# Three products in place of four in the block compression of a decoder layer

## The reference, cut to what matters

```python
def compress(rows, pos_emb, w1, w2):          # rows (L, 2 groups, 64); w1 (32*64, 256)
    L = rows.shape[0]
    nb = (L - CMP_BLK) // CMP_STRIDE + 1       # blocks of 32 rows, one every 16
    idx = np.arange(nb)[:, None] * CMP_STRIDE + np.arange(CMP_BLK)[None, :]
    blk = rows[idx] + pos_emb[None, :, None, :]
    blk = blk.transpose(0, 2, 1, 3).reshape(nb, KV_GROUPS, CMP_BLK * HEAD_DIM)
    return jax.nn.gelu(blk @ w1) @ w2
```

## Time and profile before

| | us |
|---|---|
| median of 3 runs | 2141.8 (2141.19 to 2146.41) |
| the profiled execution | 2143.66 |
| its span | 2142.0 |
| TensorE busy | 2000.0, 93% of the span |
| VectorE, ScalarE, GpSimd busy | 815.1, 636.2, 599.9 |
| matmuls of L1085, 1152 records | 248.2 busy |
| mean granted clock of TensorE | 0.966 of 2.4 GHz |

### The profile page before, as it was taken

How to read it: one execution, slowest core, us unless ns; L and a number is a source line. 1 busy time by engine, 2 the same in 40 slices (tenths; PEclk the granted TensorE clock), 3 DMA queues, 4 the chain that set the end, 5 groups by cost and what they waited for, 6 DMA issues and landing times. The chain is left out here.

```text
span 2142.0 us, 32815 instructions
## 1 busy us (share of the span) xinstructions
PE 2000.0 (93%) x11749; PEld 1737.9 (81%) x11749; DVE 815.1 (38%) x1590; ACT 636.2 (30%) x1290; POOL 599.9 (28%) x628
## 2 busy tenths in 40 slices
PE   6999989977999999869998889899999999999997
PEld 5777767856777777557887768699999999999987
DVE  5644443464343344466787743210111101110115
ACT  4311111112233343346777742222101111111112
POOL 0111111211222222154456631133322333223330
PEclk9999989988999999968999989999999999999999
DMA  5111101247787873470000022211111111111123
GB/s 182 50 80 40 40 12 63 83 130 115 118 105 101 100 101 55 77 135 11 11 11 21 2 99 89 71 45 43 49 49 41 47 49 43 45 49 49 45 64 120
DMA packets 173850, 141.35 MB, mean 66 GB/s; under 512 B 16602, under 2 KB 160683, under 8 KB 173411
## 3 DMA queue, kind: packets, MB, share of 16 engines
q1 hardware_dynamic: 169634, 131.43, 26.9%
q0 software_dynamic: 4096, 8.40, 2.6%
HBM read 124.27 MB, written 19.69 MB: 67 GB/s over the span
## 5 line engine op out<-in xcount | busy, mean ns | idle before, releaser
L392 PE MATMUL banks<-halves 128*128 128x344 f32 (+4 forms) x5184 | 856.5, 327 | 14.4 <-POOL halves L401 14.4
L392 PEld LDWEIGHTS banks<-halves 128*128 128x128 f32 (+1 forms) x5184 | 821.9, 188 | 45.2 <-POOL halves L401 8.0
L401 POOL TENSOR_TENSOR halves<-core,halves 128x1024 fp32r<-128x1024 f32 (+1 forms) x143 | 243.8, 1712 | 576.0 <-ACT halves L397 426.0
L392 PE MATMUL banks<-hidden 128*128 128x512 f32 (+3 forms) x1512 | 349.3, 387 | 9.0 <-DVE hidden L401 9.0
L392 PEld LDWEIGHTS banks<-hidden 128*128 128x128 f32 (+1 forms) x1512 | 254.4, 179 | 77.4 <-issue 9.6
L1085 PE MATMUL banks<-arena,blocks 128*128 128x254 f32 (+1 forms) x1152 | 248.2, 372 | 9.1 <-ACT arena L1219 5.1
L1085 PEld LDWEIGHTS banks<-arena,blocks 128*128 128x128 f32 x1152 | 209.5, 194 | 34.4 <-issue 6.1
L397 ACT ACTIVATE halves<-core 128x1024 fp32r<-128x1024 f32 (+1 forms) x85 | 88.2, 1047 | 390.2 <-PE banks L392 369.6
L2060 DVE TENSOR_TENSOR core<-banks,core 128x344 f32<-128x344 f32 x66 | 34.1, 517 | 441.0 <-PE banks L392 441.0
L1650 POOL TENSOR_SCALAR arena<-arena,kept 128x64 f32<-128x64 f32 (+8 forms) x192 | 122.9, 653 | 119.3 <-DVE arena L1702 117.7
L983 POOL DMA_DIRECT2D arena<-in_cache_kv x128 | 67.9, 530 | 232.9 <-PE banks L1129 206.0
(11 more groups left out here) (209 smaller groups left out, 1859.1 us busy)
## 6 DMA issues: line engine op xcount, KB each, us to landing
core<-in_cache_kv SPq DMA_DIRECT2D x128, 128.0 KB, 5.5
core<-in_w_gate SPq DMA_DIRECT2D x22, 512.0 KB, 3.8
core<-in_w_up SPq DMA_DIRECT2D x22, 512.0 KB, 3.8
core<-in_x_prompt SPq DMA_DIRECT2D x16, 512.0 KB, 3.4
arena<-in_cache_kv SPq DMA_DIRECT2D x128, 64.0 KB, 5.8
arena<-in_cache_kv POOLq DMA_DIRECT2D x128, 64.0 KB, 4.8
retention<-in_w_in SPq DMA_DIRECT2D x16, 448.0 KB, 6.4
core<-in_w_down SPq DMA_DIRECT2D x16, 448.0 KB, 3.7
```

The source lines that it names most:

```text
L392: done = pe.matmul(out, left[a], right[b], start=(first and i == 0), stop=(last and i == 2))
L401: return engine.tensor_tensor(lo, x, hi.bitcast(F32), ALU.subtract)
```

## The change

Write a chunk with an even number as x0 and the odd one after it as x1. The block that starts at the even chunk is W0 x0 + W1 x1, the one that starts at the odd chunk is W0 x1 + W1 x0', x0' being the next even chunk. After the change TensorE makes three products over pairs of chunks: P1 = W0 x1, P0 = W1 x0 and both = (W0 + W1)(x0 + x1). The even block is both - P1 - P0, the odd block is P1 + P0 of the next pair. Each product is 64 pairs by two groups, 128 columns (64 in the prompt), so there are 48 matmuls in place of 32.

Who does what: GpSimd adds W0 + W1 once for keys and once for values (`weight_sum`), and x0 + x1 for each of the four parts of each compression (`chunk_sums`, four additions of 128x256). TensorE multiplies the sum of part i-1 (`shared`) behind the two products of part i. ScalarE copies the products from PSUM (`keep_apart`), VectorE makes the two blocks of each pair in three operations (`summed`), and ScalarE's gelu reads these. Blocks now stand in the order even, odd, so the mask and the importance sum are laid out for that. `compressed(q-1)` and `importance(q-1)` move behind `shared(0)`.

The lists are written anew. On GpSimd:

```diff
+            regroup(0, 0)
+            regroup(0, 1)
+            pool.wait_ge(s["b_w_first"], 64)
+            weight_sum(0)
+            for step in STEPS_B:
+                for kv in range(2):
+                    if step in SEQS_B:
+                        chunk_sums(step, kv)
+                    if step == 0 and kv == 0:
+                        weight_sum(1)
...
+                    if step + 1 in SEQS_B:
+                        regroup(step + 1, kv)
+                if 1 <= step - 1 <= NB_SEQ:
+                    load_values(step - 1)
```

```diff
+            def chunk_sums(q, kv):
+                mc = chunks_of(q) // 2
+                for i in range(4):
+                    pool.wait_ge(s["b_kept_act"], kept_by(TURN_AT["kv"[kv], q, i] + 1, False))
+                    out, x0, x1 = (x.rearrange("p (h j) g c -> p j h g c", h=2)[:, i, :, :, 0:mc] for x in (m.both, even, odd))
+                    pool.tensor_tensor(out, x0, x1, ALU.add).then_inc(s["b_both"], 1)
```

On TensorE, in `compress`:

```diff
+                def shared(i):
+                    if q == 0 and i == 0:
+                        pe.wait_ge(s["b_w_sum"], kv + 1)
+                    pe.wait_ge(s["b_both"], 8 * q + 4 * kv + i + 1)
+                    for j in (i, 4 + i):
+                        for mt in range(2):
+                            last = product(3, P * mt, m.w1sum[kv][:, j, :], m.both, j, mt, j == mt == 0)
+                    return last
...
+                wait(pe, "b_apart", 2 * (2 * q + kv))
                 for i in range(4):
                     if i in (1, 2):
                         turn_rows(i + 1)
...
+                    for j in (i, 4 + i):
                         for mt in range(2):
+                            product(2, P * mt, m.w1[kv][:, j, :], odd, j, mt, j == mt == 0)
+                            last = product(2, 256 + P * mt, m.w1[kv][:, 8 + j, :], even, j, mt, False)
...
+                    if i:
+                        shared(i - 1)
+                    if i == 1 and kv == 0 and q:
+                        compressed(q - 1)
...
+                shared(3).then_inc(s["b_hidden"], 1)
```

On ScalarE:

```diff
+            def keep_apart(q, kv):
+                n = 2 * q + kv
+                act.wait_ge(s["b_apart_done"], n + 1)
+                wait(act, "b_summed", n)
+                act.activation(products(m.apart[:, 0:512], q), products(m.banks[:, 2, :], q), ACT.Copy).then_inc(s["b_apart"], 1)
+                act.wait_ge(s["b_hidden"], n + 1)
+                act.activation(products(m.apart[:, 512:768], q), products(m.banks[:, 3, 0:256], q), ACT.Copy
+                               ).then_inc(s["b_apart"], 1)
...
             def gelu(q, kv):
+                act.wait_ge(s["b_summed"], 2 * q + kv + 1)
...
                 if step in SEQS_B:
+                    keep_apart(step, 0)
                     gelu(step, 0)
+                if step == 0:
+                    act.wait_ge(s["r_ssum"], 1)
+                    act.activation(rms, ss, ACT.Sqrt, bias=m.small[0:NR, 64:65], scale=1.0 / HD
+                                   ).then_inc(s["r_srms"], 1)
...
+                    keep_apart(q, 1)
+                    if q + 1 in SEQS_B:
+                        keep_turned(q + 1, 0, range(2))
                     gelu(q, 1)
                     if q + 1 in SEQS_B:
+                        keep_turned(q + 1, 0, range(2, 4))
```

On VectorE:

```diff
+            def summed(q, kv):
+                n, last = 2 * q + kv, chunks_of(q) // 2 - 1
+                dve.wait_ge(s["b_apart"], 2 * n + 2)
+                wait(dve, "b_gelu", 2 * n)
...
+                dve.tensor_tensor(second[:, :, 0:last], p1[:, :, 0:last], p0[:, :, 1:last + 1], ALU.add)
+                own.after(dve.tensor_tensor(first, both, p1, ALU.subtract))
+                dve.tensor_tensor(first, first, p0, ALU.subtract).then_inc(s["b_summed"], 1)
...
+            for hp in range(4):
+                norm_sums(hp)
+            sample_out()
+            summed(0, 0)
+            sample_state()
+            summed(0, 1)
+            for hp in range(4):
+                norm_gate(hp)
             dve.wait_ge(s["r_gated"], 4)
+            summed(1, 0)
+            summed(1, 1)
```

More of the change, by code:

```diff
@@ L265, in place_mixer @@
     w1k = e(4096)
+    m.w1sum = [e(2048).rearrange("p (k n) -> p k n", k=8) for _ in range(2)]
+    m.apart, m.hidden = e(768), e(512).rearrange("p (e n) -> p e n", e=2)
     sel = b(4096)
@@ L280, in place_mixer @@
     m.rrow = x(512)
-    m.G = [b(508).rearrange("p (m n) -> p m n", m=2) for i in range(2)]
+    m.G = [b(512).rearrange("p (m n) -> p m n", m=2) for i in range(2)]
     m.brow = b(256)
@@ L883, in stage_sequences, with products @@
     qk, ss, rms, rstd = (m.rst[0:NR, 64 + j:65 + j] for j in range(4))
+    even, odd = (m.XT[:, 1024 * e:1024 * e + 1024].rearrange("p (j g c) -> p j g c", j=8, g=2) for e in range(2))
+    def products(ap, q):
+        return ap.rearrange("p (a c) -> p a c", c=64)[:, :, 0:chunks_of(q) // 2]
     def free_turn_bank(eng, i):
@@ L1067, in turn_rows, with product @@
                     last.then_inc(s["b_turned"], 1)
+                def product(bank, at, w, x, j, mt, first):
+                    out = m.banks[:, bank, at:at + P].rearrange("p (g c) -> p g c", g=2)[:, :, 0:mc]
+                    return pe.matmul(out, w[:, P * mt:P * mt + P], x[:, j, :, 0:mc], start=first, stop=(j == 7),
+                                     skip_group_check=True)
+                def shared(i):
[6 more added lines that the diff above has]
+                    return last
+                mc = nch // 2
                 turn_rows(0)
                 turn_rows(1)
[L1071 to L1076, removed]
+                wait(pe, "b_apart", 2 * (2 * q + kv))
                 for i in range(4):
@@ L1312, in _, with norm_sums @@
             dve.memset(m.vcbP, 0.0).then_inc(s["b_cleared"], 1)
-            for hp in range(4):
+            dve.memset(m.hidden, 0.0).then_inc(s["b_cleared"], 1)
+            dve.wait_ge(s["b_cleared"], 3)
+            def summed(q, kv):
+                n, last = 2 * q + kv, chunks_of(q) // 2 - 1
+                dve.wait_ge(s["b_apart"], 2 * n + 2)
+                wait(dve, "b_gelu", 2 * n)
+                p1, p0, both = (products(m.apart[:, 256 * x:256 * x + 256], q) for x in range(3))
+                first, second = (products(m.hidden[:, e, :], q) for e in range(2))
+                dve.tensor_tensor(second[:, :, 0:last], p1[:, :, 0:last], p0[:, :, 1:last + 1], ALU.add)
+                own.after(dve.tensor_tensor(first, both, p1, ALU.subtract))
+                dve.tensor_tensor(first, first, p0, ALU.subtract).then_inc(s["b_summed"], 1)
+            def norm_sums(hp):
                 o, sums = m.oall[hp], m.rst[:, 16 * hp:16 * hp + 16]
@@ L1334, in _ @@
[L1334 to L1340, removed]
@@ new lines, in sample_state @@
+            def sample_state():
+                own.after(dve.tensor_tensor(S2v, rk8.unsqueeze(2).broadcast_to(S2v.shape),
+                                            rv.unsqueeze(1).broadcast_to(S2v.shape), ALU.mult))
+                dve.wait_ge(s["r_srms"], 1)
+                own.after(dve.reciprocal(rstd, rms))
+                dve.scalar_tensor_tensor(out=ro, in0=ro, scalar=rstd, in1=rg, op0=ALU.mult, op1=ALU.mult
+                                         ).then_inc(s["r_o"], 1)
+                dve.scalar_tensor_tensor(out=S0, in0=S0, scalar=m.gone[0:NR, :], in1=S2, op0=ALU.mult,
+                                         op1=ALU.add).then_inc(s["r_new_state"], 1)
@@ L1399, in _ @@
                         keep_output(q)
+                if step == 2:
+                    summed(2, 0)
                 q = step - 1
@@ L1436, in _ @@
                     own.after(added)
+                    if step in SEQS_B:
+                        summed(step, 1)
                     dve.tensor_reduce(bst[:, 5:6], SR[:, SEL], AX.X, ALU.max, negate=True).then_inc(s["b_sel_max"], 1)
```

116 lines of the change are left out of this document (58 added, 58 removed).

## The result

| | before | after |
|---|---|---|
| median, us (4 runs each, on one chip) | 2141.73 | 2236.22 (2233.69 to 2238.7) |
| ratio to before | 1 | 1.0424, 95% interval [1.0391, 1.0458] |
| the profiled execution, its span, us | 2143.66, 2142.0 | 2237.12, 2235.4 |
| TensorE busy, mean granted clock | 2000.0, 0.966 | 2002.0, 0.934 |
| compress(2, 1) starts, C of step 2 | 573.71 | 619.68 |

Slower, as forecast, by 94.5 us where 79 had been worked out. The stretch up to the attention explains nearly all: 92.4 of the 93.4 us between the spans. TensorE is not busy for less time although it has a quarter fewer columns to multiply in the sequences' compressions; what it saves comes back as records at half clock.

A forecast was written before the change was run, and what follows sets the result against it. TensorE's own work was taken to bound the stage. Losses of 35.9 (start), 39.9 (period), 1.5 (end) and 2 (low clock) sum to 79.3 us, giving 2223 for the profiled execution and a forecast of 2222; own range 2206 to 2238.

The forecast's parts named there:

- The mechanism: GpSimd's page reads and DMAs delay chunk sums each step; VectorE's constants wait delays the start; both hold TensorE; 60%.
- three signs of being wrong: A period under 49; table reads starting before the last sum's release; TensorE at compress(0,1) before 529.
- The period's term: Steps 2 to 8: GpSimd's late chunk sums lengthen each of six periods from 48.90 to 55.5 us, 39.9 lost.
- The start's term: Up to compress(2,1): VectorE's wait for constants holds ScalarE and that TensorE; compress(2,1) starts 35.9 us late.
- The failed step: compress(0,1) after TensorE's idling: 7.2+0.4 us starting at half clock, then 7.5 at full clock, done at 547.8.
- The end: Step 8: the values' products wait for later page loads, 1.5 us lost, and about 2 for low clock.
- (1): Rival: the clock stays up after TensorE's idling; as the forecast but 25 us less, 2198 us; chance 12%.
- (2): Rival: GpSimd reads the table entries ahead of the waiting sums; period 45.8, 2160 us; chance 10%.
- (3): Rival: GpSimd is in time, only VectorE's hold at the start remains; period 43.0, 2143 us; chance 4%.
- (5): Rival: page loads on SyncE and GpSimd slip too, each 3 us a period costing 18; 2243 and more; 6%.
- (4): Rival: TensorE's columns in the compression's matmuls alone set the end; 5.9 us a period saved, about 2104; 8%.

The follow-up runs named there:

- e1: The change with GpSimd's page-table reads and page loads moved to mid step, round the keys' regroup: 2166.18 us, ratio 1.010.
- e8: e1 without the chunk sums, the shared product reading the even chunks alone: 2165.71 us, ratio 1.011.
- e5: The change with the prompt's products run over 128 columns, zeros in the unused half, in place of 64: 2215.14 us, ratio 1.0329.
- e6: e1 with VectorE's start reordered (summed(0,0) and norm gates before sample_out) and ScalarE's square root later: 2157.23 us, ratio 1.0055.
- e7: e6 together with the 128-column prompt products of e5: 2153.85 us, ratio 1.0049.
- e9: e7 with SyncE's third-sequence table reads earlier, ScalarE's square root earlier, and VectorE's sample_state before summed(1,0): 2130.85 us, ratio 0.9937.
- e4: The change without the chunk sums, the shared product reading the even chunks alone, GpSimd's other order kept: 2194.7 us, ratio 1.0242.
- e3: The change with VectorE doing both prompt sums before the sample tokens and ScalarE's square root behind step 0's gelu: 2220.8 us, ratio 1.0361.

## Why the prediction was right, and where its sizes were off

**The mechanism held, at both places.** Period, from C = 733.82: last sum released C+8.4 (forecast 8.15), first DMA C+17.9 (17.6), sums C+28.0 (27.4), shared(0) C+28.8 (28.4), small transposes C+40.9 (41.7), next C at C+56.3 (55.5). The wait is 9.31 for 9.3. None of the three signs of being wrong came: the period is far over 49, the reads started at 742.3 behind the release at 742.22, and compress(0,1) started behind 529. e1 takes the wait away by order alone, so GpSimd's queue is shown as its cause, and e8 shows that the additions' own time is not.

**The period's term, 39.9, measured 44.8.** Two parts of about 2.4 each. The first period is 58.0: the first of its DMAs starts at C+20.0 and the wait is 11.35. The other five average 56.0, and the low clock lasts longer in them than worked out, in one of two ways. In two of them, as in the step shown, it ends before the 56 records, but a second stretch of half clock lies in the tail, values and scores, which takes 15.4 us where 13.8 had been read. It follows the wait of 0.83 at the small transposes; e1 has that wait in the fence above, and 1.97 and 4.21 behind it. In the other three the low clock behind the long wait lasts into the 56 records (7.56 to 8.25 us for 6.42), the small transposes start without a wait at C+41.6 to C+42.4, and the tail takes 13.8. The forecast had put the low clock only behind the long wait, for 5.9 us.

**The start's term, 35.9, measured 46.0**, of which 1.3 was there when the stage began. The failed step is "two product turns 7.2+0.4, then 64 records and a transpose at full, 7.5". These records stayed at half clock, and so did those of compress(0,0) before them, so that the idle stretch began some 7 us later than with wide records (e5); it was 29.12 and not 38. From its first record compress(0,1) took 21.3 us where 15.1 had been worked out. Its bias took 9.16, not 7.1. And the first 16 records of compress(1,1) ran at half clock behind a wait of 2.42 us, 3.55 for 2.02, which the forecast had at full. That is 6.2, 2.1 and 1.5 of the 10.1. With wide records (e5) the idle stretch is 36.06, compress(1,0) starts at 554.53 (forecast 555.9) and C of step 2 is 34.6 behind, close to the 35.9: the rest of that working was right. The records' price of 0.112 was right at 128 columns and at the full clock; for the prompt's 64 columns the forecast had bounded it by weights' size and not by the clock.

**The end, 3.5, measured 1.7** at the start of the attention; the values' products started at C+32.2 (forecast 31.6).

**Sum.** 1.3 that the stage began with, 44.7, 44.8, 1.7, and 0.9 for the rest, 93.4. Against 79.3 the start has 10.1 more, the period 4.9, the rest 0.9, the end 1.8 less. So 2236.22 lies near the upper end of the forecast's own 2206 to 2238, and not by errors that cancel: the terms that were off were nearly all too small, and the clock is the reason for most of it.

**The rivals.** (1) fell with the clock of 0.86 in 700 to 750, (2) with the start of the reads at 742.3, (3) with the wait of 9.31; the arrangement that (3) describes is e1's, and it took 2166 for 2143. (5), slipping page loads, was not needed here but is what e6 and e7 ran into once the start was repaired. (4), 2104, TensorE's columns alone, is not reached even by e9: its period of 44.8 is 1.8 above the 43.0 (48.9 less 5.9), worth 11 us, and its start 9.9 later than before where that rival had 4 gained. Its quickest periods are 44.0; they hold a wait of 0.66 us for gelu before the product with w2 and one of 0.83 before the small transposes, where it was 0.23.

What stays open: why half clock follows a wait of 0.8 us in some steps and not in others (in e7, the 32 records behind such a wait at 769.76 took 3.68 us, full clock).

## What to carry to other kernels

Before giving work to an idle engine, write out its list from the event that the new consumer waits on, and count everything that stands ahead, register reads and DMA issues too: the 18 us of reads and loads a step hold next to nobody in one order and cost 70 us in the other. When a hold is removed, look at once for what is next in the same list and in the queues that feed it; here there were three behind one another (VectorE's constants, its next sum, SyncE's pages). Leaving out the wait (e4) gave 42 us where moving its cause gave 70, since the cause held a second place.

## What the runs showed of the hardware

Float32 products with 64 columns and 128-column weights, with a few transposes between, ran at a granted clock of 0.50 through 21 us in which TensorE was never idle (532.9 to 554.2), at 0.214 us a record. In e3 the clock fell from 1.00 to 0.50 in such records behind 2.29 us of idling. With 128 columns the clock rose while the second product turn ran, and a record then took 0.112 (e5). Half the columns cost twice the time.

The 16 reads of page numbers on GpSimd began with the release of the chunk sum ahead of them (742.3), ran while that sum and a copy of 2.76 us were at work, and took nearly as long as the 16 DMAs that they feed, 8.7 us for 9.8. They do not count as busy time.
